# Last block of queries in a fused transformer layer: the three local visits first, then the feed-forward's fourth row operand and first weights, over the local visits' weights

## The reference, cut to what matters

```python
h = rms_norm(x, g_attn)
proj = h @ w_in                               # queries, keys, values of three head groups
out_a = swa_sink_attention(...)               # 8 heads, window of two chunks
out_b = mla_attention(...)                    # 4 heads, chunk-causal over all 2048 keys
out_m = memory_attention(...)                 # 4 heads, 256 memory tokens
x = x + concatenate([out_a, out_b, out_m]) @ w_o
hf = rms_norm(x, g_ffn)
x = x + square(relu(hf @ w_ff1)) @ w_ff2      # 1024 -> 4096 -> 1024
```

## Time and profile before

| | us |
|---|---|
| median of 3 runs | 2150.13 (2148.4 to 2151.18) |
| the profiled execution | 2148.57 |
| its span, first to last instruction | 2146.8 |
| PE busy (matmuls) | 2100.2, 98% of the span |
| DVE, ACT, POOL busy | 1410.4, 1044.0, 1110.7 |
| mean granted TensorE clock | 0.995 |

### The profile page before, as it was taken

The page is one execution under the profiler, slowest core; times in us unless marked ns, Lnnn a source line. Parts: engine busy times, 40 slices in busy tenths (PEclk is TensorE's granted clock), DMA queues, the critical chain, the costliest instruction groups (busy, mean ns, idle before and its releaser), DMA issues.

```text
span 2146.8 us, 30840 instructions
## 1 busy us (share of the span) xinstructions
PE 2100.2 (98%) x9992; PEld 1739.0 (81%) x9992; DVE 1410.4 (66%) x2095; ACT 1044.0 (49%) x1870; POOL 1110.7 (52%) x899
## 2 busy tenths in 40 slices
PE   8999999899999999989999999999999999999999
PEld 6899999777777777778888878888888888888887
DVE  5788888977666655596666786666635644354463
ACT  6566666567777767643333543333323233222221
POOL 2666666646575757586666686666346700020220
PEclk9999999999999999999999999999999999999999
DMA  7133243688585756764444744444677752244363
GB/s 250 40 113 94 84 115 119 207 241 263 173 258 182 222 180 198 252 204 154 158 161 162 248 158 162 161 142 138 230 245 265 258 193 98 98 137 141 134 220 113
DMA packets 293439, 374.20 MB, mean 174 GB/s; under 512 B 27149, under 2 KB 187117, under 8 KB 291518
## 3 DMA queue, kind: packets, MB, share of 16 engines
q1 hardware_dynamic: 293310, 372.56, 54.0%
HBM read 247.28 MB, written 125.19 MB: 174 GB/s over the span
## 4 chain that ended last, share of the span: by engine, by line
PE 55%; issue 0%; DVE 0%
PE bank L128 55%; DVE f_w_lo L1888 0%; DVE f_r L2164 0%
## 5 line engine op out<-in xcount | busy, mean ns | idle before, releaser
L128 PE MATMUL bank<-f_t_hi,f_w_hi 128*128 128x512 f32 x896 | 349.5, 390 | 10.7 <-issue 4.4
L128 PE MATMUL bank<-f_t_hi,f_w_lo 128*128 128x512 f32 x896 | 348.7, 389 | 0.0
L128 PE MATMUL bank<-f_t_lo,f_w_hi 128*128 128x512 f32 x896 | 348.6, 389 | 0.0
L128 PE MATMUL bank<-f_w_lo,f_a_hi 128*128 128x512 f32 x896 | 348.6, 389 | 0.0
L128 PE MATMUL bank<-f_w_hi,f_a_hi 128*128 128x512 f32 x896 | 348.5, 389 | 0.0
L128 PE MATMUL bank<-f_w_hi,f_a_lo 128*128 128x512 f32 x896 | 348.5, 389 | 0.0
L2764 POOL TENSOR_TENSOR a_p_lo<-a_prob,a_p_hi 128x512 fp32r<-128x512 f32 (+1 forms) x192 | 233.3, 1226 | 151.5 <-DVE a_p_hi L2928 55.1
L2041 POOL TENSOR_TENSOR f_r<-f_r,f_y 128x512 f32<-128x512 f32 x24 | 42.1, 1787 | 325.4 <-DMA f_r<-s_x 325.4
L128 PEld LDWEIGHTS bank<-f_t_hi,f_w_hi 128*128 128x128 f32 x896 | 168.2, 188 | 49.1 <-issue 12.2
L2143 DVE TENSOR_TENSOR f_a_lo<-f_a_raw,f_a_hi 128x1024 fp32r<-128x1024 f32 x112 | 158.3, 1414 | 71.8 <-ACT f_a_hi L2066 71.5
L128 PEld LDWEIGHTS bank<-f_t_hi,f_w_lo 128*128 128x128 f32 x896 | 168.2, 188 | 35.2
(11 more groups left out here) (350 smaller groups left out, 4826.8 us busy)
## 6 DMA issues: line engine op xcount, KB each, us to landing
f_a_raw<-s_aop SPq DMA_DIRECT2D x112, 512.0 KB, 4.4
w_raw<-in_w_ff SPq DMA_DIRECT2D x64, 512.0 KB, 5.3
s_aop<-f_a SPq DMA_DIRECT2D x128, 256.0 KB, 4.4
s_aop<-f_s SPq DMA_DIRECT2D x96, 256.0 KB, 2.3
f_w_raw<-in_w_ff SPq DMA_DIRECT2D x64, 256.0 KB, 5.9
f_t_raw<-s_hop SPq DMA_DIRECT2D x14, 1024.0 KB, 8.4
f_r<-in_w_ff SPq DMA_DIRECT2D x48, 256.0 KB, 6.2
a_vals<-s_v SPq DMA_DIRECT2D x40, 264.0 KB, 4.7
```

The source lines that it names most:

```text
L128: ins = pe.matmul(out, a, b, start=(first and j == 0), stop=(last and j == n - 1))
```

## The change

Three things move, and no instruction is added or removed:

1. In the last block of queries all local visits go first: (13,0) (14,0) (15,0) (8,1) (9,1) (10,1) (11,1). So tile 8's square to transposes come 11 slots later (square from 148 to 159), 9's, 10's and 11's 10 each; tile 11's square goes from slot 179 to 189, its norm to 190, its transposes from 182 and 183 to 192 and 193, its sums from 185 to 195, its stores from 187 and 189 to 197 and 199.
2. Behind the last local visit (`local_end` = slot 149) P2's row operand is loaded (slot 149), split by ACT at slot 155 and by DVE at 157 and 159, over the local visits' weights; before it was loaded at 198 and split at 218 and 216.
3. The raw weights of unit 0 are loaded at slot 150 in place of 199, and wait for the last local visit's product instead of `scaled`. Splitting them and making their sums stays in its slots.

```diff
@@ the order of visits @@
-            take = other if other and begin >= ready[u - 1] and (len(other) >= len(local) or not local) else local
+            take = other if other and begin >= ready[u - 1] and (len(other) >= len(local) and u < NU - 1 or not local) else local
@@ the table @@
-    for j in range(len(F["t_hi"])):
+    last_local = LOCAL[-1]
+    local_end = portion_slot[(last_local + 1) * 2 * KH - 1] + 3
+    assert local_end + 12 < N
+    put("t_load", local_end, P2)
+    for j in (P1, P6, P5):
         put("t_load", N + LAG + 2, j)
-    put("w1_load", scale_slot[-1] + 2, 0)
+    put("w1_load", local_end + 1, 0)
     put("w1_load", tail + 8, 1)
-    for j, (high, lows) in enumerate(((-5, (-1, 3)), (-3, (7, 10)), (-1, (13, 14)), (17, (15, 15)))):
-        put("t_high", tail + high, j)
+    for j, high, lows in ((P2, local_end + 6, (local_end + 8, local_end + 10)), (P1, tail - 5, (tail - 1, tail + 3)),
+                          (P6, tail - 3, (tail + 7, tail + 10)), (P5, tail - 1, (tail + 13, tail + 14))):
+        put("t_high", high, j)
         for part, s in enumerate(lows):
-            put("t_low", tail + s, (j, part))
+            put("t_low", s, (j, part))
@@ SP @@
             for j in of("t_load", s):
-                sp.wait_ge(pv_done, N)
+                if j == P2:
+                    sp.wait_ge(y_made, 2 * last_local + 2)
+                else:
+                    sp.wait_ge(pv_done, N)
...
             for n in of("w1_load", s):
                 if n == 0:
+                    sp.wait_ge(y_made, 2 * last_local + 2)
+                else:
                     sp.wait_ge(scaled, NUNITS // 2)
@@ counters: P2 is now the first split @@
+FIRST_SPLITS = (P2, P1, P6, P5, P7, P4, P3)
-            wait(pe, t_lo_done, NOPS * u.p + j + 1)
+            wait(pe, t_lo_done, NOPS * u.p + (j if u.p else FIRST_SPLITS.index(j)) + 1)
-                dve.wait_ge(F["t_hi_done"], j + 1)
+                dve.wait_ge(F["t_hi_done"], FIRST_SPLITS.index(j) + 1)
```

## The result

The changed kernel is slower: median 2156.7 us (2154.61 to 2160.74, nine runs) against 2149.59 (2147.81 to 2151.18, nine), ratio 1.0034 with the interval 1.0026 to 1.0042, so 7.1 us. Its profiled execution took 2158.22 us (span 2156.4), 9.6 more than that of before. The forecast was 2151.4 in a range to 2155.6: the time lies outside it.

A forecast was written before the change was run, and what follows sets the result against it. PE, busy 98%, was taken to bound the kernel, so only its waits count. Losses +1.9 and +1.9 less gain 2.5 made +1.3 us: 2149.9 profiled, a median of 2151.4, range 2146.8 to 2155.6.

The forecast's parts named there:

- The bound: Whole kernel: PE busy 98% of the span, so the change can only add or remove PE's waits.
- The gain: Feed-forward's start: P2's split leaves, shortening PE's waits before P2 and P7; 2.5 us, bounds 1.8 and 4.8.
- P7 can start near 923.7: Feed-forward's start: P7 starts there in place of 925.77, 2.0 us sooner, after DVE's low part of 2.3 us.
- my 4.5 us: Feed-forward's start: the gain if DVE and POOL exclude each other whole, freeing two POOL operations; not adopted.
- Weights and the middle: Early loads of weights and P2's rows, and P2's split in the middle of the block: 0 us each.
- Rival 3: Middle of the block: the early split on ACT and DVE is not free; +1.5 us, 2152.9, chance 0.10.
- The first loss: Attention's end: tile 11's square and norm delay the last exponentials and the tail; +1.9 us, bounds +0.5 and +3.5.
- PE comes to step 188 some 0.8 us earlier: Attention's end: eight transposes moved behind step 188 bring PE there 0.8 us sooner, spent at once.
- The second loss: Tail: loads behind tile 11's sums delay P1's rows and PE's operands; +1.9 us, bounds 0 and +3.
- rival 2: Seam around 884: PE's idleness lowers the clock; 3.5 us on top of the sum, 2154.9, chance 0.20.
- My bound of 3: Tail: upper bound, +3 us, on the loss from loads queued behind tile 11's sums.
- Rivals 1 and 4: 1: the seam hides, 2148.6, chance 0.20; 4: P7's rows land too late, both losses stay, 2153.9, chance 0.10.

The follow-up runs named there:

- weights_late: spread_free with unit 0's raw weights loaded at slot 199 as before the change; 2148.1 us, ratio 0.9992 to the kernel before.
- visits_only: The kernel before with only the order of visits changed, P2's rows and unit 0's weights loaded and split as before; 2157.02 us, ratio 1.0035.
- tile11_tail: The changed kernel with tile 11's square, norm and transposes moved behind the attention, its sums and stores behind the loads; 2151.39 us, ratio 1.0007 to before.
- square_back: spread_free with tile 11's square back between the exponentials of steps 189 and 190, its norm left behind the attention; 2148.83 us, ratio 0.9996 to before.
- stores_behind: The changed kernel with tile 11's three stores behind the loads of P1, P6 and P5 in SP's queue; 2151.52 us, ratio 1.0011 to before.
- stores_ahead: spread_free with tile 11's stores put back around the loads, ahead of P1's load in SP's queue; 2156.23 us, ratio 1.0029 to before.
- the fills: Matmuls that nothing reads put into PE's waits: nine before tile 11's transposes in stores_behind (2151.02 us), and fill_both (2155.36 us).
- own_banks: tile11_tail with tile 11's transposes earlier, in two free banks, and the second early tail visit behind the spreads; 2148.42 us, ratio 0.9997 to before.
- spread_free: own_banks, but the last heads' spreads on PE no longer wait for DVE's takes of tile 11's transposes; 2148.57 us, ratio 0.9993 to before.
- fill_both: The changed kernel with nine unread matmuls before tile 11's transposes and twelve before the tail's second portions; 2155.36 us, ratio 1.0023 to before.

## Why the prediction was wrong, step by step

**The bound** was right: PE busy 98%, and the time is its waits and its clock.

**The gain (2.5, measured 1.8).** P2's wait goes, P7's nearly, the other three stay, as said. From P6's product to the end mark the changed kernel takes 35.95 us, before 37.76. What fails is "P7 can start near 923.7" with 0.5 us beyond. I had asked what is late next and looked only at ACT and at P7's rows. DVE sat idle for 3.28 us of what it had saved, until POOL's last sum of tile 13 let it take tile 15, and P7's low part then took 3.22 us where I had put 2.3:

```profile
930.26 1.29 DVE L2903 TENSOR_TENSOR a_hT<-bank,a_g_col 128x512 f32<-128x512 f32 x2 [3.28 <-POOL a_tsum L2798]
931.47 3.22 DVE L2129 TENSOR_TENSOR f_t_lo<-f_t_raw,f_t_hi 128x2048 fp32r<-128x2048 f32 x1
...
928.74 1.30 POOL L2798 TENSOR_TENSOR a_tsum<-a_hT,a_tsum 128x512 f32<-128x512 f32 x1
929.99 1.30 POOL L1868 TENSOR_TENSOR w_raw<-w_raw 128x512 f32<-128x512 f32 x1
```

The meeting of POOL and DVE that I had weighed was worth 0.97 us: L1868, the L1867 of before, took 1.30 us in place of 2.27. I had set that against a DVE half of some 2 us, but the half was itself held up. In the trace of before POOL's L2787 ran from 917.29 to 919.45 and DVE's second half from 918.22 to 920.53, 2.31 us where such a half takes 1.21 alone (L3012 at 920.64 now): it lost the time up to the end of L2787. L1867 came at 919.41, when 1.1 us of that half were left, and lost about these. Here the second to come waited for the rest of the first, in both directions. The Trainium skill, "SBUF — State Buffer", "Who interferes with whom", calls the ports that the two share an exclusive lock; the trace agrees, and my 4.5 us did not follow from the page: I had charged each meeting with a duration that held a wait already.

**Weights and the middle (0 and 0).** Right within 0.3 us: weights_late, and visits_only, which has neither and comes to step 189 only 0.26 us sooner. Rival 3 is out.

**The first loss (1.9, measured 3.4).** The chain was the right one. Its start was 0.9 us wrong: "PE comes to step 188 some 0.8 us earlier" was +0.1 (the scores of step 189 at 876.61 before, 879.31 now, less 2.58). The gain of the moved transposes is real at the end (the tail of tile11_tail starts 1.1 us early) but not yet at step 189. So the last exponential ended, less 2.58, at 884.15 and not at 883.0; from there to the tail I had 2.9 us and it took 3.3. Against tile11_tail the change starts its tail 4.5 us later: 1.17 are the square (square_back); the rest is norm, transposes and some 0.7 of slow clock (visits_only, without it, is 0.73 ahead of the change there), which no run takes apart further. All this lies at my upper bound of 3.5.

**The second loss (1.9, measured 5.4).** This is the step that failed. From the tail's first product to P6's the changed kernel takes 35.76 us, before 30.32. I had the place and the path, and mis-sized the term twice. The issue came 2 us later than 888.6 (893.19 less 2.58), since POOL's sums came with the late chain. (My own terms, 885.3 and twice 1.3 and twice 0.5, give 888.9.) And I let the rows land 5.3 us after it, as a constant; they took 7.8 (tile view of the rows), where the trace of before had 4.9 and stores_behind 4.6. Just ahead of them tile 13's rows and two stores had been issued; with the two stores but without tile 13's rows ahead it was 6.3 (stores_ahead). That they are the reason fits and was not tested. So PE waited 2.94 us for the low parts and not 1.2, while the 0.7 before tile 12's transposes did not come. The other half of the term was missing: the sum had the clock at nothing and left it to rival 2. Half the clock for the 3.4 us behind this wait and for the last 1.1 us of the first fall, which lie behind the tail's start, is 2.3 us by an estimate from the rows; with the 2.94 that makes 5.2 of the 5.4.

My bound of 3 came from a worry about cover and not from the worst of these. stores_ahead shows how wrong the frame was: with the rest of the seam clean the same order of the queue costs 8.5 us. The two losses are not a sum: taking this one out of the change gives back 3.4 (stores_behind), leaving it alone costs 8.5, so behind a tail that is late already more than half of it is hidden.

**Rival 2** came true, at both waits. I gave it 0.2 though my own chain had PE busy for 1 us of 4, like the two stretches that I had shown beside it; such a rival needs more than that. I had read their falls too short as well: finer stretches of the trace of before give 3.4 us behind 404 and 10.2 behind 438, not 2.8 and 9. Its price is the part that stays open: 3.4 us at half the clock each time, where the fills gave back 0.5 (medians) to 2 us (traces) for the first wait in stores_behind, and for both together 1.3 in the medians and nothing in the traces.

**Rivals 1 and 4** are out: both losses came, each above its forecast, and P7's rows were in time.

## What to carry to other kernels

A job that is moved takes its followers along in every queue. List for each queue what now stands behind a wait that it did not stand behind, and ask what the thing behind it feeds: here a 0.5 us store that waited for POOL held the load on which ACT, DVE and PE hung in a row, and cost 3.4 us here and 8.5 where nothing else was late. Price a late load from its latency in a full queue, not in the queue of before, and do not add delays of one chain as if they were apart. A late operation on an engine that is idle half the time can still be the last link: the places to keep free of long operations are the short masked steps at a unit's end.

## What the hardware showed that I had not expected

The wait that lets the clock fall is not told by its length. 2.32 us of it brought 3.4 us at a granted clock of 0.5 in the changed kernel and none in visits_only, 2.53 us none in tile11_tail, 2.30 us 6.8 in stores_behind, 6.17 us the same 6.8 in stores_ahead, and 2.07 us before P4 brought 3.4 in own_banks. Each of these is one trace. The Trainium skill, "TensorE: Matmul & The Clock Gate", Part 1, says of a kernel's start that how many matmuls run slow varies between runs of one kernel. No kernel here has two traces that could show it; the mean granted clocks of the 29 runs of before that stand beside spread_free go from 0.993 to 0.996, which fits and is all that is on record.

A small operation on POOL is no fixed price either: the one of one column ahead of a norm took 0.19 us in the changed kernel at 910.31, 1.14 in tile11_tail and 1.11 in fill_both, the last two beside a low part on DVE, and each ended as that low part did (901.51 and 901.46 in tile11_tail, 909.22 and 909.17 in fill_both). And filling a wait with idle matmuls may only move it: PE came sooner to the next late operand.
